# Half-array matmuls in alternating order, and the shared 64 KB at the low end of SBUF

## The reference

```
for l in range(2):
    x = x + 0.5 * g1 * swiglu(mod(norm(x)), w_in, w_out)          # FFN, inner width 2816
    u = mod(norm(x))
    merged = sum_i sigmoid(gate_i(u)) * (mixer_i(u) @ w_up_i)     # three mixers
    x = x + g2 * merged @ w_out
    x = x + 0.5 * g3 * swiglu(mod(norm(x)), w_in, w_out)
return norm(x)
```

## Time and profile before

| | us |
|---|---|
| median of three runs | 2577.58 |
| the profiled execution | 2577.9 |
| its span, first to last instruction | 2576.2 |
| PE busy in the span | 2474.7 |
| DVE busy | 1337.3 |
| ACT busy | 889.2 |

### The profile page before, as it was taken

How to read it: one execution, slowest core, us unless ns; L and a number is a source line. 1 busy time by engine, 2 the same in 40 slices (tenths; PEclk the granted TensorE clock), 3 DMA queues, 4 the chain that set the end, 5 groups by cost and what they waited for, 6 DMA issues and landing times.

```text
span 2576.2 us, 32310 instructions
## 1 busy us (share of the span) xinstructions
PE 2474.7 (96%) x11908; PEld 2007.0 (78%) x11908; DVE 1337.3 (52%) x1799; ACT 889.2 (35%) x1270; POOL 92.2 (4%) x163
## 2 busy tenths in 40 slices
PE   3999999999999999999989999999999999999998
PEld 3888887788777778888878888877886777788886
DVE  6553556565465754433355545566554566543333
ACT  3431333422255444213344223243223554432222
POOL 2000000000000000000000000000000000000000
PEclk9999999999999999999999999999999999999999
DMA  7564562211213424422235545422112233343231
GB/s 278 188 213 145 181 212 81 81 65 62 87 42 118 157 90 147 163 98 100 96 107 195 197 154 200 168 74 67 69 62 70 91 128 130 111 151 129 90 105 58
DMA packets 93004, 319.24 MB, mean 124 GB/s; under 512 B 11824, under 2 KB 12208, under 8 KB 92784
## 3 DMA queue, kind: packets, MB, share of 16 engines
q1 hardware_dynamic: 57888, 215.87, 24.3%
q0 software_dynamic: 21200, 76.95, 9.0%
q10 hardware_dynamic: 13824, 25.17, 2.8%
HBM read 303.27 MB, written 14.68 MB: 123 GB/s over the span
## 4 chain that ended last, share of the span: by engine, by line
PE 89%; DVE 6%; ACT 3%; issue 1%; DMA 1%; SPq 0%; DVEq 0%; ACTq 0%
PE PS L402 73%; PE PS L414 3%; PE PS L795 3%; PE PS L607 1%; PE PS L618 1%; PE PS L621 1%; DVE ada L1617 1%; DVE wl L1151 1%; ACT wh L848 1%; PE PS L568 1%; ACT sco L1038 1%; PE PS L674 0%; PE PS L670 0%; PE PS L685 0%; DMA ada<-in_ada_w_dram 0%
## 5 line engine op out<-in xcount | busy, mean ns | idle before, releaser
L1151 DVE TENSOR_TENSOR wl<-raw,wh 128x1024 fp32r<-128x1024 f32 (+2 forms) x360 | 466.1, 1295 | 803.2 <-ACT wh L848 802.8
L402 PE MATMUL PS<-uh,wh 128*128 128x512 f32 x2144 | 858.2, 400 | 13.2 <-DVE wl L1151 11.0
L402 PE MATMUL PS<-uh,wl 128*128 128x512 f32 x2144 | 837.8, 391 | 0.0
L402 PE MATMUL PS<-ul,wh 128*128 128x512 f32 x2144 | 837.2, 390 | 0.0
L848 ACT ACTIVATE wh<-raw 128x1024 fp32r<-128x1024 f32 (+2 forms) x360 | 401.6, 1116 | 932.7 <-PE PS L402 902.4
L402 PEld LDWEIGHTS PS<-uh,wh 128*128 128x128 f32 x2144 | 403.9, 188 | 109.2 <-issue 17.0
L402 PEld LDWEIGHTS PS<-uh,wl 128*128 128x128 f32 x2144 | 403.5, 188 | 85.8
L402 PEld LDWEIGHTS PS<-ul,wh 128*128 128x128 f32 x2144 | 404.2, 189 | 81.0 <-issue 2.9
L402 PE MATMUL PS<-hh,wl 128*128 128x512 f32 x704 | 277.4, 394 | 0.0
L402 PE MATMUL PS<-hh,wh 128*128 128x512 f32 x704 | 277.4, 394 | 0.0
L402 PE MATMUL PS<-hl,wh 128*128 128x512 f32 x704 | 277.4, 394 | 0.0
(11 more groups left out here) (226 smaller groups left out, 2126.1 us busy)
## 6 DMA issues: line engine op xcount, KB each, us to landing
raw<-in_ffn_in_dram SPq DMA_DIRECT2D x176, 512.0 KB, 3.5
ada_raw<-in_ada_w_dram POOLq DMA_DIRECT2D x144, 512.0 KB, 3.8
raw<-in_mix_in_dram SPq DMA_DIRECT2D x88, 512.0 KB, 3.5
raw<-in_ffn_out_dram SPq DMA_DIRECT2D x32, 768.0 KB, 4.3
raw<-in_ffn_out_dram SPq DMA_DIRECT2D x32, 640.0 KB, 3.9
g_in<-gates_dram ACTq DMA_DIRECT2D x48, 256.0 KB, 3.1
ada<-in_ada_w_dram SPq DMA_DIRECT2D x16, 512.0 KB, 11.0
raw<-in_mix_up_dram SPq DMA_DIRECT2D x16, 512.0 KB, 3.5
```

Of the source, the lines that this page charges most:

```text
L402: mm = e.matmul(PS[:, bank, :], w[:, j % 2, k * P:(k + 1) * P], v[:, k, :], start=(k == 0 and w is wh and v is xh), stop=(k == K - 1 and w ...
L1151: TTo(wl[:, j % 2, 0:K * P], raw[:, j, 0:K * P], wh[:, j % 2, 0:K * P], ALU.subtract)\
```

## The change

Two edits at once.

The matmuls that use half of the array are issued so that neighbours use different halves. In the output stage of mixer B all 16 products with `intra` now come first, and then all 32 with the states; only the first tile's products begin a new sum in their bank, the others write columns that have not been written yet. In mixer C's and A's value products the loop over key tiles moves outside the loop over halves. No product is added or left out, and the instruction streams of DVE, ACT, POOL and SP are the same as before.

The 64 KB that the stages share move to the low end: `A0` becomes 16512, and everything else moves up by 65536 (`uh` 98432, `ul` 114816, `wh` 155776, `wl` 168064). `hh`, `oh` and all other tiles of the shared 64 KB now begin on multiples of 128 bytes, too.

```diff
+HALVES_IN_TURN = (0, 2, 1, 3)
...
+        A0 = base[0]
+        base[0] += 65536
         x = place("x", [P, KD, SEQ], F32)
...
         sq = place("sq", [P, 2, SEQ], F32)
-        A0 = base[0]
         h32 = place("h32", [P, 2, SEQ], F32, A0 + 57344)
...
                     c0, c1 = t * P, (t + 1) * P
-                    for par in range(2):
-                        r = slice(64 * par, 64 * par + 64)
-                        for x2 in range(2):
-                            for pair in range(2):
+                    for x2 in range(2):
+                        for pair in range(2):
+                            for par in range(2):
+                                r = slice(64 * par, 64 * par + 64)
                                 rhs = bp[r, (2 if x2 == 0 else 0) + pair, c0:c1]
                                 mm = e.matmul(PS[:, 2 + par, (2 * x2 + pair) * P:(2 * x2 + pair + 1) * P],
                                               bp[r, 2 + pair, c0:c1], rhs, start=True, stop=True)
...
-                    for s in range(4):
+                    for s in HALVES_IN_TURN:
                         par, pair = s // 2, s % 2
                         mm = e.matmul(PS[64 * par:64 * par + 64, 5, 256 + pair * P:256 + (pair + 1) * P],
                                       k_beta[:, s, :], Um[:, s, :], start=True, stop=True)
... (the same line in the two products of the scan, L652 and L660)
                 e.wait_ge(qe_done.sem, qe_done.at(l, TT))
                 for t in range(TT):
-                    for s in range(4):
+                    for s in HALVES_IN_TURN:
                         par, pair = s // 2, s % 2
                         r = slice(64 * par, 64 * par + 64)
                         e.matmul(PS[r, 6 + pair, t * P:(t + 1) * P], u_val[:, t, s, :], intra[:, t, s, :],
-                                 start=True, stop=True)
-                        for ch in range(2):
-                            n = 2 * t + ch
-                            mm = e.matmul(PS[r, 6 + pair, n * CHUNK:(n + 1) * CHUNK], st[r, n, pair, :],
-                                          bp[r, pair, n * CHUNK:(n + 1) * CHUNK], start=False, stop=True,
-                                          skip_group_check=True)
+                                 start=t == 0, stop=True, skip_group_check=True)
+                for n in range(NCH):
+                    for s in HALVES_IN_TURN:
+                        par, pair = s // 2, s % 2
+                        r = slice(64 * par, 64 * par + 64)
+                        mm = e.matmul(PS[r, 6 + pair, n * CHUNK:(n + 1) * CHUNK], st[r, n, pair, :],
+                                      bp[r, pair, n * CHUNK:(n + 1) * CHUNK], start=False, stop=True,
+                                      skip_group_check=True)
                 mm.then_inc(o_mm.sem, 1)
...
                 def scores_c(t):
-                    for h in range(8):
+                    for h in (0, 4, 1, 5, 2, 6, 3, 7):
...
-                    for kv in range(2):
-                        for z, kt in enumerate(kts):
+                    for z, kt in enumerate(kts):
+                        for kv in range(2):
                             mm = e.matmul(PS[64 * kv:64 * kv + 64, 6, :], v_tok[:, t - 1 + kt, 64 * kv:64 * kv + 64],
                                           pT[:, 2 * kt + kv, :], start=(z == 0), stop=(z == len(kts) - 1))
...
-                    for h in range(4):
-                        r = slice(64 * (h % 2), 64 * (h % 2) + 64)
+                    for two in range(2):
                         for kt in range(t + 1):
-                            mm = e.matmul(PS[r, 6, (h // 2) * P:(h // 2 + 1) * P], v_tok[:, kt, h * HEAD:(h + 1) * HEAD],
-                                          pT[:, kt, h * P:(h + 1) * P], start=(kt == 0), stop=(kt == t))
+                            for h in (2 * two, 2 * two + 1):
+                                r = slice(64 * (h % 2), 64 * (h % 2) + 64)
+                                mm = e.matmul(PS[r, 6, two * P:(two + 1) * P], v_tok[:, kt, h * HEAD:(h + 1) * HEAD],
+                                              pT[:, kt, h * P:(h + 1) * P], start=(kt == 0), stop=(kt == t))
```

More of the change, by code:

```diff
@@ L169, in encoder_kernel @@
         up_m = place("up_m", [P, 5, SEQ], F32, W0 + 12288)
-        assert A0 + 65536 <= 229368, A0 + 65536
+        assert base[0] <= 229368, base[0]
         PS = ctx.enter_context(nc.psum_tensor("PS", [P, 8, SEQ], F32))
```

## The result

| | before | changed |
|---|---|---|
| median of four runs, us | 2577.73 | 2535.22 |
| lowest to highest | 2574.92 to 2579.16 | 2533.63 to 2536.48 |
| profiled execution, and its span | 2577.9, 2576.2 | 2533.63, 2531.9 |

The ratio is 0.9836, 95% interval 0.9819 to 0.9853: 42.5 us faster, where 2536.0 us was forecast. The lines named here lie 5 to 10 further down in the changed kernel: L402 is L407, L568 is L573, L637 L642, L652 L657, L670 L677, L674 L683, L685 L694, L695 L704, L740 L749, L780 L790, L795 L805.

What follows compares the result with a forecast made beforehand. PE, busy 96% of the span, was taken to bound the kernel. Order 25.9 us, less 0.6 for the clock, plus address 16.6 gave 41.9 off 2577.9: 2536.0 us, own range 2529 to 2542, stated range 2527 to 2557.

Steps and rivals of the forecast that it cites:

- The address, 16.6 us: 2496 matmuls moving from the shared 64 KB go from 233.3 to 226.7 ns steps once aligned and low: 16.6 us.
- Rival B: The address does nothing, the slow step belongs to something else in those stages: 2552.6 us; chance 0.13.
- Rival C: Fast step belongs to low addresses, weights' too, so all dense matmuls turn slow: 2597.4 us (milder form 2580.8); chance 0.13.
- Rival D: Order gives less: output stage saves only 4.1 us, or a second half-clock stretch comes: 2546.8 us; chance 0.12.
- Outcome by the rule against the address: By the skill pages an operand's address costs nothing, so the address edit is worth nothing; the outcome is rival B.
- The alternating rate: Half-array runs cost 0.28 us fixed plus 0.106 us a product per 128 columns; L568 saves 4.6 us, later scores 3.9.
- Places with runs of two: L740, L637, L652 and L660: runs of two in a half already overlap with the other half's; saves nothing.
- L780, 1.0 of 1.8: Value products: t=3 saves 0.59 us, t=2 0.3, t=1 already fast; 1.8 us over two layers.
- The output stage, 7.84 of 7.8: Mixer B's output stage falls from 11.75 to 3.95 us, saving 7.8 us twice, 15.6 us; bounds 4.1 and 8.65.
- The wait ahead of L740: Savings in `scores_c(0)` and `scores_c(1)` only lengthen PE's wait before the first value product to about 3.5 us: counted at nothing.
- The 0.3 us a layer: Allowance for a further half-clock stretch behind the wait before the first value product: 0.3 us a layer, 0.6 in all.

Runs made afterwards that it cites:

- `a3_high_128`: The kernel before, with the shared 64 KB moved by 64 bytes to 157824, a multiple of 128, still at the high end; 2561.82 us (0.9936).
- `a4_low_64`: The kernel before, with the shared 64 KB at the low end, 64 bytes past a multiple of 128; 2577.14 us (0.9997).
- `d1_all_64`: The changed kernel with every tensor 64 bytes past a multiple of 128, `hh` and `hl` 256 bytes further against the weights; 2535.06 us (0.9832).
- `b1_u_64`: The changed kernel with `uh` and `ul` 64 bytes past a multiple of 128, the weights moved by 128; 2584.73 us against 2577.57 before (1.0028).
- `a2_address_only`: The kernel before, old order, with only `A0` moved to the low end (16512); 2562.91 us against 2577.23 before (0.9939).
- `b2_w_64`: The changed kernel with the weights `wh` and `wl` 64 bytes past a multiple of 128; 2587.15 us against 2577.57 before (1.0045).
- `c3_without_free`: The changed kernel with the old order at L637, L652, L660, L740 and the scores of mixer C's first two tiles; 2537.73 us (0.984).
- `c2_halves_in_runs`: The changed kernel, output stage's kinds still apart, but each kind all in the first half of the array, then the second; 2541.42 us (0.9855).
- `c1_kinds_in_turn`: The changed kernel with each output-stage slot's `intra` product again followed by its two state products, slots alternating halves; 2552.13 us (0.9903).
- `a1_order_only`: The changed kernel with `A0` back at the high end (157760), so only the new order; 2555.33 us against 2577.23 before (0.9911).

## Why the prediction was right, point by point

- **The address, 16.6 us.** Right in its size: the FFN-out stretches are 528 matmuls each and 3.5 us shorter, four times, the two up projections 1.2 us each, together 16.6. The reason was half right. The prediction took it for alignment, not place, and `a3_high_128` with `a4_low_64` show that. It took the unit for 128 bytes and the operand for the moving one alone, and argued 16 columns as 64 bytes. That step is wrong: `d1_all_64` is fast with no tile on a multiple of 128, and `b1_u_64` slow with both tiles on one. The forecast was saved by the edit keeping `uh` and `wh` together (both moved by 65536) and putting `hh` at the same remainder modulo 256.
- **Rival B** (nothing) is out by `a2_address_only`. **Rival C** is out in its mechanism, low against high. That the weights' address counts, which it also said, is right: `b2_w_64` lost 52 us by 64 bytes. Its hint, the two durations of L512 (396 and 388 ns), does not follow from the distance, since `ab_hi` and `ab_lo` have the same one; it stays open, as said above.
- **Rival D** (the order gives less) is out: the output stage takes 3.91 us, and no second stretch at half clock came behind the wait.
- **Outcome by the rule against the address:** the Trainium skill ("SBUF — State Buffer", Who interferes with whom) says that PE never waits on anyone at SBUF. The rows of the table at other distances than 0 disagree, by 6 to 8 ns a matmul. The 216 ns that the prediction quotes from "TensorE: Matmul & The Clock Gate", Back-to-back issue gap, is that section's figure for an isolated matmul; for a stream with a weight load before each it gives about 131 ns. No run here shows either.
- **The alternating rate**, 0.28 us and 0.106 us a product per 128 columns: L573 1.16 (forecast 1.13), scores 2.00 (1.98), L790 1.53 at t = 2 (before 1.80, of which 0.3 were to go) and 1.97 at t = 3 (1.98). L573 moved everything behind it by 0.55 us at each of six places; at t = 0, partly at half clock, by 0.82 and 0.37. In sum 4.5 of 4.6. The scores of tiles 2 and 3: 0.97 each of 0.98. Places with runs of two: unchanged, as `c3_without_free` also says. L677's 16 take 1.97 us, against 3.33 in runs of one half (`c2_halves_in_runs`). The Trainium skill ("TensorE: Matmul & The Clock Gate", What overlaps and what doesn't) lets weight loads overlap only where the row groups differ; this row disagrees, since these products share all rows.
- **L780, 1.0 of 1.8: here a term of the sum was wrong.** The prediction put the whole saving of the value products on the path. At t = 3 they are 0.6 us shorter, but the up projections behind them wait for DVE's `ol`, and that wait grew from 0.93 to 1.33 us, so only 0.2 us a layer is left. With 0.27 for t = 2 and 0.05 for t = 1 it is 0.5 us a layer. PE's group in the changed kernel; before, the waits of both layers were 1.9 us together:

```profile
L805 PE MATMUL PS<-oh,wh 128*128 128x512 f32 x128 | 50.1, 391 | 2.7 <-DVE ol L1576 2.7
```

- **The output stage, 7.84 of 7.8.** The number came out, but the reason was incomplete. The prediction counted every product at the alternating rate and gave a change of kind no price of its own. Its lower bound, "if nothing overlapped", 7.6 us, saves 4.1, is in effect the case of `c2_halves_in_runs`: 6.95 us, saves 4.8. It took no account of the changes of kind undoing the overlap, as `c1_kinds_in_turn` shows they do. Had the change only alternated, the same working would have been wrong by 15.7 us.
- **The wait ahead of L740.** The saving of the first two score stages is indeed absorbed, but not in one wait of 3.5 us. PE now waits at three places. The first is the row of L704 above (0.78 us, before 0.23); the others in the timeline of PE:

```profile
707.85 0.51 PE L407 MATMUL PS<-uh,wh 128*128 128x512 f32 x1 [0.77 <-ACT pc L934]
...
717.13 1.10 PE L749 MATMUL PS<-pT,v_tok 128*64 128x512 f32 x4 [2.61 <-ACT pT L1040]
```

What I had missed is that ACT copies a projection's result (L934) only behind the eight exponentials of the tile (L1048), and PE's next projection needs that bank. ACT, the last exponential and the copy, which ends 0.04 us before PE starts:

```profile
706.74 0.39 ACT L1048 ACTIVATE sco<-sco,mx 128x128 f32<-128x128 f32 x1
...
707.23 0.58 ACT L934 ACTIVATE pc<-PS 128x512 f32<-128x512 f32 x1
```

With the waits split like this the last one grew by 0.13 us only, and no second stretch at half clock came: ten matmuls in the 3.4 us behind it, against nine. The 0.3 us a layer for it were not needed.

```profile
718.10:721.50 3.40, 3.40 (x10) 2.67 (x9) 3.30 (x6) 1.03 (x3) 0.00 (x0) 0.50 0.00 0
```

- **What the sum left out.** The profiled execution won 44.3 us, 2.4 more than the forecast. By 63 us the changed kernel is 3.2 us ahead, for which the sum had no term: 0.2 us before the first matmul, 1.4 where the clock rose to full speed sooner (45 to 49 us), and 1.6 where the kernel before had a second stretch at half clock (its window from 57 to 63 us has a mean clock of 0.72; 13 matmuls) and the changed one had none:

```profile
57.00:63.00 6.00, 4.47 (x13) 3.55 (x14) 3.28 (x4) 3.59 (x5) 0.00 (x0) 0.72 0.34 104
```

```profile
57.00:63.00 6.00, 6.00 (x27) 4.94 (x28) 3.65 (x6) 2.33 (x4) 0.00 (x0) 1.00 0.58 173
```

`c2_halves_in_runs`, with the new address, has this stretch again, so it belongs to neither edit. On the other side PE waited 0.7 us ahead of L781 in the second layer for nothing that the profile names; the kernel before has no such wait, and each of the twelve experiments has one of 0.3 to 1.3 us. 41.9 + 3.2 + 0.6 for the clock that was not lost - 0.8 for L780 - 0.7 is 44.2 of the 44.3 us. Without the 3.2 us, which neither edit brought, the profiled execution would have been 0.8 us short of the forecast instead of 2.4 above it.

## What to carry to other kernels

Read the distance between starts of one kind of matmul stage by stage; where two stages of the same shape differ by some per cent, compare the addresses of both operands, modulo 256 here, before thinking of engines. Put products of one array shape in a run, and within the run alternate the halves: alternation between unlike shapes brought nothing. Ask of each saving what wait stands behind it: 0.4 of the last value products' 0.6 us went into a wait for DVE. A price that comes out right still needs the experiment that takes its reason away, as here with the two halves of the output stage.

## What the runs showed of the hardware

- A stream of fp32r matmuls with new weights each (128 by 128 against 512 columns) has a step of 226.7 ns when moving rows and weights begin at the same address modulo 256, and 232.4, 233.3 and 234.3 ns at distances of 128, -64 and -96 bytes, also while DVE, ACT and POOL do nothing. With weights of 8 columns distance 0 has 226.7 ns too, and the others a mean of 231.4. Whether the two reads collide in SBUF or are started in step, these runs don't tell.
- Where halves or quarters of the array are used, products in different halves run side by side, whether the halves are of rows (L748) or of columns (L677, L790). Runs of two products in a half overlap with the other half's next two (L740, L637); longer runs do so only around the change of half (`c2_halves_in_runs`: 109 ns from start to start in the runs, 6 to 103 ns where they meet).
- A change between 128 by 64 and 64 by 64 products costs 0.14 us by the starts of the instructions (0.16 us by the stages' times), and no overlap of the halves shows across it: 11.74 us with and 11.75 us without alternation.
- Kernels with the same work differ by some us through stretches at half clock behind the norms and at the start: over the whole profile from 65 us (`b2_w_64`) to 81 us (`a1_order_only`).
